# Two mixed layers of a float32 network: units reordered, heads taken in pairs between the k steps of gate units, convolution taps summed in PSUM

## The chip, the core and the metric

The kernel runs on one core of one Trainium2 chip. The metric is the device time of one execution in microseconds (us). The kernel before took 2114.37 us in the median of three runs (2113.19 to 2114.48).

## What is computed

A batch of one sequence of 256 tokens, width 1024, all float32, goes through two stacked networks. The first has two layers; each adds half a SwiGLU block (inner width 2816), then a hybrid mixer, then another half SwiGLU block. The second has a dilated attention mixer, a SwiGLU block, a forgetting attention mixer and a SwiGLU block. The change concerns the hybrid mixer alone, which runs twice:

```python
proj = h @ w_in + b_in                       # 1024 -> pa 1024 | pb 672 | pc 1024 | pg 3072
xa  = causal_conv4(pa[..., :512])            # LRU branch
y_a = (rg_lru(xa) * gelu(pa[..., 512:])) @ lru_w_out
q   = (rms_norm(cq) @ w_uq)                  # latent attention, 8 heads of 64 + 32 rotary
kv  = (rms_norm(ckv) @ w_ukv)
y_b = softmax_causal(q k^T) v @ mla_w_o
c   = pc[..., :512] * sigmoid(pc[..., 512:]) # convolution branch
c   = silu(layer_norm(causal_depthwise_conv31(c)))
y_c = c @ conv_w_out + conv_b_out
g   = sigmoid(pg)                            # three gates of width 1024
merged = g0 * y_a + g1 * y_b + g2 * y_c
x   = x + merged @ w_out
```

## The kernel before

**Weights.** All weights come in one stream of slots of 128 x 2048 float32 (1 MB) through three buffers. SyncE (SP) loads a slot into `raw` (`load`, L486 to L490) once the slot that had the buffer is split. ScalarE (ACT) rounds it to `whi` (`split`, L551 to L557), VectorE (DVE) makes `wlo = raw - whi` (L1018 to L1022), and TensorE (PE) forms each product as three float32r matmuls, hi x hi, hi x lo and lo x hi (`use`, L1794 to L1811). A slot is four k steps for both blocks of 128 rows: 24 matmuls of 512 columns. ACT may split slot i+2 as soon as PE is done with slot i-1.

**Order.** Every engine works through a list written out by hand, in order. ACT's and DVE's splits stand as `upto(i)` (all splits up to number i) between the other steps; where a step waits, all that stands behind it on its engine waits too. `MIX_UNITS` (L107) lists the products of a mixed layer (*units*), whose results go in turn to two pairs of PSUM banks, 0 and 1 and 2 and 3, so a unit can start when the one two before it has been read out. `MIX_TURNS` (L51) lists the groups of transposes (*turns*), which take banks 6 and 7 in turn in the same manner.

**A mixed layer.** It has 36 slots, in this order: `pa0`, `pa1` (the LRU branch's two inputs), `pb0`, `pb1` (latents), `glu`, `val` (the convolution branch's two), `uq0`, `uq1`, `uk`/`uv` (queries, keys, values), then for each branch its two gate units `g` and its two output units `y`, and last `wo0`, `wo1` (the output projection, L2184). PE's list is L2053 to L2191, ACT's L694 to L836, DVE's L1217 to L1424, POOL's (GpSimd's) L1659 to L1706. PE does the LRU gates' eight small matmuls in banks 4 and 5 (L2079), the turns of the query and key rows (`qk_turns`), and the eight heads in one run behind `g01` (`attention`, L1971 to L2043). For each head PE makes scores (L1984, L1986), DVE their largest value (L1126), ACT the exponentials with their row sums (L627), PE turns them (L1996), ACT copies them out (L618) and PE multiplies by the values (L2015), 64 columns a head. DVE divides all eight by the row sums at the end (L1119), and two more turns `o0`, `o1` bring the result to channels by tokens.

**The convolution.** It has 31 taps on 4 tiles of 128 channels x 256 tokens. DVE has tiles 0 to 2: `conv(n)` (L1228 to L1245) does n rounds of three `scalar_tensor_tensor`, with a drain ahead of each, which read the padded input and the sum in SBUF and write the sum in SBUF. POOL has tile 3: L1702 multiplies, L1705 adds, all 31 after `scan` and rotation (L1693 to L1706). PE then sums over channels for the mean and the variance (L2091).

**Gates and merging.** DVE reads out each gate unit with its bias (`biased`, L1247 to L1257) into one of two row buffers, ACT applies the sigmoid (L840), and `merge` (L1265 to L1290) multiplies an output unit by its gate and adds it to `merged`; for the third branch DVE first adds the output bias (L1281, L1284).

## Time and profile before

| what | value |
|---|---|
| median of three runs | 2114.37 us (2113.19 to 2114.48) |
| the profiled execution's own time | 2112.89 us |
| its span, first to last instruction | 2111.1 us |
| mean granted clock of TensorE | 0.985 |
| first mixed layer, from 199.5 to 464.0 us | 264.5 us |
| second mixed layer, from 837.4 to 1101.7 us | 264.3 us |

The profiled execution lies 1.8 us around its span and 1.5 us below the median. Its records of PE matmuls overlap: a matmul of 512 columns reads 0.39 us, and the next starts 0.23 us after it, so times of PE are read below from start to start and not from busy time. In the same manner VectorE's and ScalarE's records last longer than the distance to the next one.

### The profile page before, as it was taken

How to read it: one execution, taken by the hardware profiler on the slowest of the kernel's cores; microseconds unless marked ns; L12 is line 12 of the kernel's file. 1: busy time of each engine (PE TensorE's matmuls, PEld its weight loads, DVE VectorE, ACT ScalarE, POOL GpSimd, SP SyncE). 2: the span in 40 equal slices, each digit the busy share in tenths (PEclk: the TensorE clock that was granted, in tenths of full speed). 3: DMA queues.
4: the chain of work that ended last, by engine and by line, in shares of the span. 5: the costliest groups of instructions: out<-in, count | busy, mean ns of one | idle time of the engine just before them, and what ended most of it. 6: DMA issues, size and time to landing. Idle time of an engine off the chain costs nothing.

```text
span 2111.1 us, 26411 instructions
## 1 busy us (share of the span) xinstructions
PE 2035.4 (96%) x9851; PEld 1678.6 (80%) x9866; DVE 1238.3 (59%) x1366; ACT 1011.2 (48%) x1279; POOL 240.9 (11%) x357
## 2 busy tenths in 40 slices
PE   8999988999999999988999999999999999999998
PEld 6888867778888888867778887778778888888887
DVE  5555579865545555669865545555556455446554
ACT  5445664544445445664445444544445434455433
POOL 1000168000000000069000002111100000000000
PEclk9999998999999999999999999999999999999999
DMA  7554442545555555542455554444335554425552
GB/s 266 189 189 176 175 151 89 175 159 202 196 181 184 204 179 186 184 150 87 155 182 201 187 183 158 144 141 152 140 109 190 188 190 160 162 78 182 206 180 100
DMA packets 54626, 354.16 MB, mean 168 GB/s; under 512 B 7696, under 2 KB 8336, under 8 KB 12816
## 3 DMA queue, kind: packets, MB, share of 16 engines
q1 hardware_dynamic: 53968, 352.51, 47.1%
q8 instruction: 54, 0.88, 0.2%
q10 hardware_dynamic: 576, 0.53, 0.1%
q14 instruction: 28, 0.23, 0.0%
HBM read 351.97 MB, written 1.05 MB: 167 GB/s over the span
## 4 chain that ended last, share of the span: by engine, by line
PE 83%; DVE 7%; ACT 4%; DVEq 2%; issue 2%; POOL 1%; DMA 1%; POOLq 1%; SPq 0%; ACTq 0%
PE psum L1809 58%; PE psum L1860 17%; DVE wlo L1022 3%; DVE arena L1243 2%; ACT whi L557 2%; PE psum L1875 1%; DVEq L1237 1%; PE psum L1938 1%; PE psum L2230 1%; PE psum L2251 1%; DMA raw<-w_stream 1%; PE psum L2237 1%; PE psum L1821 1%; PE psum L2015 1%; POOL arena L1651 1%
## 5 line engine op out<-in xcount | busy, mean ns | idle before, releaser
L1022 DVE TENSOR_TENSOR wlo<-raw,whi 128x2048 fp32r<-128x2048 f32 x325 | 745.0, 2294 | 447.9 <-ACT whi L557 447.8
L1809 PE MATMUL psum<-whi,xTh 128*128 128x512 f32 (+1 forms) x1936 | 769.0, 397 | 14.8 <-DVE xTl L1048 5.2
L1809 PE MATMUL psum<-whi,xTl 128*128 128x512 f32 (+1 forms) x1936 | 752.9, 389 | 0.0
L1809 PE MATMUL psum<-wlo,xTh 128*128 128x512 f32 (+1 forms) x1936 | 752.8, 389 | 0.0
L557 ACT ACTIVATE whi<-raw 128x2048 fp32r<-128x2048 f32 x325 | 621.1, 1916 | 258.1 <-PE psum L1860 151.3
L1809 PEld LDWEIGHTS psum<-whi,xTh 128*128 128x128 f32 x1936 | 366.9, 190 | 93.2 <-issue 5.9
L1809 PEld LDWEIGHTS psum<-whi,xTl 128*128 128x128 f32 x1936 | 366.8, 189 | 76.3
L1809 PEld LDWEIGHTS psum<-wlo,xTh 128*128 128x128 f32 x1936 | 367.5, 190 | 69.4
L1860 PE MATMUL psum<-whi,braT 128*128 128x512 f32 x1056 | 337.7, 390 | 0.0
L1860 PEld LDWEIGHTS psum<-whi,braT 128*128 128x128 f32 x1056 | 198.3, 188 | 41.1
L1860 PE MATMUL psum<-wlo,braT 128*128 128x512 f32 x528 | 205.5, 389 | 0.0
L654 ACT ACTIVATE arena<-psum,small 128x256 f32<-128x256 f32 x132 | 55.4, 471 | 194.8 <-PE psum L1809 194.7
L659 ACT ACTIVATE braT<-psum 128x256 fp32r<-128x256 f32 x132 | 43.5, 382 | 217.2 <-PE psum L1875 217.2
L1165 DVE TENSOR_TENSOR braT<-psum,braT 128x256 fp32r<-128x256 f32 x132 | 49.9, 419 | 112.0 <-ACT braT L659 112.0
L1860 PEld LDWEIGHTS psum<-wlo,braT 128*128 128x128 f32 x528 | 99.2, 188 | 20.0
L1158 DVE SCALAR_TENSOR_TENSOR arena<-psum,small,arena 128x256 f32<-128x256 f32 x132 | 57.8, 480 | 85.0 <-ACT arena L654 84.6
L1243 DVE SCALAR_TENSOR_TENSOR arena<-arena,vec 128x256 f32<-128x256 f32 x180 | 98.7, 602 | 6.3 <-issue 1.8
L1702 POOL TENSOR_SCALAR arena<-arena,vec 128x256 f32<-128x256 f32 x60 | 77.2, 1287 | 0.3 <-issue 0.3
L1938 PE MATMUL psum<-con,arena 128*128 128x128 f32 (+2 forms) x372 | 52.7, 282 | 18.6 <-ACT arena L799 12.5
L1624 POOL TENSOR_SCALAR small<-small 128x2 f32<-128x2 f32 x9 | 1.7, 192 | 594.1 <-ACT arena L584 594.1
L1938 PEld LDWEIGHTS psum<-con,arena 128*128 128x128 f32 (+2 forms) x372 | 43.2, 136 | 28.9 <-ACT arena L799 13.5
L1809 PE MATMUL psum<-whi,latT 128*128 128x512 f32 (+1 forms) x176 | 57.3, 396 | 5.1 <-DVE wlo L1022 4.3
(236 smaller groups left out, 1449.2 us busy)
## 6 DMA issues: line engine op xcount, KB each, us to landing
raw<-w_stream SPq DMA_DIRECT2D x326, 1024.0 KB, 4.8
bias<-chunks SPq DMA_DIRECT2D x18, 256.0 KB, 5.0
x<-x_in SPq DMA_DIRECT2D x2, 512.0 KB, 5.1
raw<-w_stream SPq DMA_DIRECT2D x4, 256.0 KB, 7.3
arena<-gate_w SPq DMA_DIRECT2D x2, 512.0 KB, 5.1
arena<-fins SPq DMA_DIRECT2D x2, 512.0 KB, 5.8
con<-consts SPq DMA_DIRECT2D x1, 720.0 KB, 10.9
out<-x ACTq DMA_DIRECT2D x2, 256.0 KB, 2.3
```

The costliest lines, as they stand in the source:

```text
L557: act.activation(whi[:, r], raw[:, r], ACT.Copy).then_inc(hi_done, 1)
L654: act.activation(f_sg[:, rb], gate_up(b, j)[:, rb, 0:256], ACT.Silu, scale=rs[:, rb:rb + 1]).then_inc(silu_done, 1)
L659: act.activation(h_of(b, j, 0)[:, :, rb * P:(rb + 1) * P], psum[:, 6 + rb, 0:256].rearrange("p (t s) -> p t s", s=P), ACT.Copy).then_inc(t ...
L1022: TT(wlo[:, r], raw[:, r], whi[:, r].bitcast(F32), ALU.subtract).then_inc(lo_done, 1)
L1158: ins = STT(f_h[:, rb], gate_up(b, j)[:, rb, 256:512], rs[:, rb:rb + 1], f_sg[:, rb], ALU.mult, ALU.mult)
L1165: TT(h_of(b, j, 1)[:, :, rows], psum[:, 6 + rb, 0:256].rearrange("p (t s) -> p t s", s=P), h_of(b, j, 0)[:, :, rows].bitcast(F32), ALU.sub ...
L1237: dve.drain()
L1243: ins = STT(cacc[:, t], cpad[:, t, k:k + S], w, cacc[:, t], ALU.mult, ALU.add)
L1702: TS(products[:, k % 2, t - CONV_DVE], window, w, None, ALU.mult)
L1809: ins = pe.matmul(dst(rb), s(kt)[:, rows], w[:, r, at_:at_ + cols], start=start and n == 0 and k == 0, stop=stop and n == len(kts) - 1 and ...
L1860: ins = pe.matmul(pair(c)[:, rb], s[:, t, rows], w[:, r, t * D + c * W:t * D + (c + 1) * W], start=start and t == 0 and k == 0, stop=stop ...
L1938: ins = pe.transpose(dst[0:rows.shape[1], col:col + P], rows, ident)
```

## The change

- **Order of units.** `glu` and `val` come first, then `pa0`, `pa1`, `pb0`, `pb1`, `g00`, `uq0`, `uq1`, `uk`, `uv`, `g01`, `y00`, `y01`, `g10`, `g11`, `g20`, `g21`, and then `y10`, `y11`, `y20`, `y21` and the output projection. The weight stream is laid out to match. The turns follow, and `o0`, `o1` are gone.
- **Hooks.** Turns, scores, turns of probabilities, the products with the values, and the sums over channels are issued from hooks ahead of single k steps of the large units (`{4: [turn_p(0)], ...}`: number of k step and what stands before it).
- **Heads.** They go in four pairs. ACT also multiplies the probabilities by the reciprocal row sums (`normed`) before they are turned. The product with the values (`pv`) puts both heads of a pair into one bank with channels on the partitions, and ACT and DVE split it straight into `latT` (`o_hi`, `o_lo`).
- **Taps.** DVE's taps keep their sums in PSUM banks 4 and 5 and write SBUF only in the last round; they start after `val`. The LRU gates go to banks 6 and 7. POOL does 11 of its 31 taps ahead of the rotation and 20 after it.
- **Gate rows** have four buffers. The bias of the third branch times its gate is added to `merged` by POOL (`with_conv_bias`), not by DVE.
- **Output projection.** Its four slots go k half by k half (`wo0`, `wo1`, `wo0`, `wo1`). `uk`'s product signals on its own (`uk_in`).

The core of the diff:

```diff
-MIX_UNITS = [("pa0", 2, "act"), ("pa1", 2, "act"), ("pb0", 2, "dve"), ("pb1", 1, "dve"),
-             ("glu", 2, "act"), ("val", 2, "act"), ("uq0", 1, "act"), ("uq1", 1, "act"), ("uk", 1, "act"), ("uv", 0, "act"),
-             ("g00", 2, "dve"), ("g01", 2, "dve"), ("y00", 1, "dve"), ("y01", 1, "dve"),
-             ("g10", 2, "dve"), ("g11", 2, "dve"), ("y10", 1, "dve"), ("y11", 1, "dve"),
-             ("g20", 2, "dve"), ("g21", 2, "dve"), ("y20", 1, "dve"), ("y21", 1, "dve"),
+MIX_UNITS = [("glu", 2, "act"), ("val", 2, "act"), ("pa0", 2, "act"), ("pa1", 2, "act"), ("pb0", 2, "dve"), ("pb1", 1, "dve"),
+             ("g00", 2, "dve"), ("uq0", 1, "act"), ("uq1", 1, "act"), ("uk", 1, "act"), ("uv", 0, "act"),
+             ("g01", 2, "dve"), ("y00", 1, "dve"), ("y01", 1, "dve"),
+             ("g10", 2, "dve"), ("g11", 2, "dve"), ("g20", 2, "dve"), ("g21", 2, "dve"),
+             ("y10", 1, "dve"), ("y11", 1, "dve"), ("y20", 1, "dve"), ("y21", 1, "dve"),
...
+                def normed(p):
+                    act.wait_ge(mla_rden, M * MPAIRS + p + 1)
+                    for h in (2 * p, 2 * p + 1):
+                        for rb in range(RB):
+                            ins = act.activation(pm[h % 2][rb], pm[h % 2][rb], ACT.Copy, scale=rden[:, rb * NH + h:rb * NH + h + 1])
+                        ins.then_inc(mla_normed, 1)
...
+                def o_hi(p):
+                    act.wait_ge(mla_pv, M * MPAIRS + p + 1)
+                    act.activation(latT[:, 0, p], psum[:, 6, 0:S], ACT.Copy).then_inc(mla_hi, 1)
...
+                upto(15)
                 rows("uv", [v_row[:, rb] for rb in range(RB)], rs4[:, 2:4])
+                upto(16)
+                gate_sigmoid(b, 0)
                 act.wait_ge(ya_f, M + 1)
                 act.activation(braT[:, 0], gel, ACT.Copy).then_inc(ya_hi, 1)
                 upto(17)
+                qk_out(0)
+                qk_out(1)
+                upto(18)
+                qk_out(2)
+                qk_out(3)
                 gate_sigmoid(b, 1)
                 upto(19)
+                exp(0)
+                normed(0)
+                upto(20)
+                turned_out(0)
                 upto(21)
+                o_hi(0)
+                exp(1)
+                normed(1)
+                upto(22)
+                turned_out(1)
+                o_hi(1)
                 upto(23)
+                exp(2)
+                normed(2)
+                upto(24)
+                turned_out(2)
+                upto(25)
+                o_hi(2)
+                exp(3)
+                normed(3)
 
...
-                            w = vec_("dww", k * 4 + t)
+                            w, acc = vec_("dww", k * 4 + t), conv_acc(t)
                             if k == 0:
-                                ins = TS(cacc[:, t], cpad[:, t, 0:S], w, vec_("dwb", t), ALU.mult, ALU.add)
+                                if t == 0:
+                                    dve.drain()
+                                ins = TS(acc, cpad[:, t, 0:S], w, vec_("dwb", t), ALU.mult, ALU.add)
                             else:
-                                ins = STT(cacc[:, t], cpad[:, t, k:k + S], w, cacc[:, t], ALU.mult, ALU.add)
+                                ins = STT(cacc[:, t] if k == TAPS - 1 else acc, cpad[:, t, k:k + S], w, acc, ALU.mult, ALU.add)
                         if k == TAPS - 1:
                             ins.then_inc(conv_done, 1)
...
+                conv(1)
+                upto(5)
+                conv(2)
+                upto(6)
+                conv(2)
+                dve.wait_ge(xpad_in, M + 1)
+                lru_conv((0, 1))
+                upto(7)
+                lru_conv((2, 3))
+                upto(8)
+                conv(1)
+                upto(9)
+                conv(1)
+                biased("pb0", 0, [pb[:, rb, 0:W] for rb in range(RB)])
+                upto(10)
+                conv(1)
+                biased("pb1", 1, [pb[:, rb, W:] for rb in range(RB)])
+                dve.sem_inc(lat_row, 1)
+                upto(11)
+                conv(3)
+                for n, t0, tn in ((0, 0, 2), (1, 2, 1), (2, 3, 1), (3, 4, 1)):
+                    lo_turns(b, plan, f"lat{n}", latT[:, 1, t0:t0 + tn], latT[:, 0, t0:t0 + tn], [vec_("q_norm", t) for t in range(t0, t0 + tn)])
+                    if n == 1:
+                        conv(1)
+                        upto(12)
+                gate(0)
+                upto(13)
+                conv(1)
                 dve.wait_ge(sqrt_done, M + 1)
                 STT(gr, ltmp, 1.0, gr, ALU.add, ALU.mult)
+                upto(14)
                 dve.drain()
                 dve.wait_ge(ix_done, M + 1)
                 TT(gi, gr, gi, ALU.mult)
                 for t in range(4):
                     ins = dve.tensor_tensor_scan(gr[:, t], ltmp[:, t], gi[:, t], 0.0, ALU.mult, ALU.add)
                 ins.then_inc(scan_done, 1)
+                upto(15)
+                conv(3)
+                upto(16)
                 dve.wait_ge(ya_hi, M + 1)
                 TT(braT[:, 1], gel, braT[:, 0].bitcast(F32), ALU.subtract).then_inc(ya_lo, 1)
+                conv(1)
+                upto(17)
                 conv(2)
+                gate(1)
                 upto(18)
                 conv(2)
                 merge(0)
+                conv(1)
+                largest(0)
+                conv(1)
+                reciprocals(0)
                 upto(19)
+                conv(1)
                 merge(1)
+                upto(20)
+                conv(1)
+                o_lo(0)
+                upto(21)
+                largest(1)
+                conv(1)
+                reciprocals(1)
+                gate(2)
+                upto(22)
+                conv(1)
+                o_lo(1)
                 conv(2)
+                largest(2)
+                upto(23)
+                reciprocals(2)
+                gate(3)
+                upto(24)
                 conv(2)
+                o_lo(2)
+                conv(1)
+                largest(3)
                 upto(25)
+                reciprocals(3)
+                gate(4)
...
+                merge(2)
+                merge(3)
                 upto(30)
                 merge(4)
+                upto(31)
+                for n in range(2):
                     lo_turns(b, plan, f"m{n}", xTl[:, 2 * n:2 * n + 2], xTh[:, 2 * n:2 * n + 2])
+                merge(5)
+                upto(32)
+                upto(33)
+                for n in range(2, 4):
+                    lo_turns(b, plan, f"m{n}", xTl[:, 2 * n:2 * n + 2], xTh[:, 2 * n:2 * n + 2])
+                upto(34)
+                ready = lambda c, rb: dve.wait_ge(slot_used, b.slot + 35 + c)
                 residual(units.place("wo0"), 1.0, ready, ((0, 0), (0, 1)))
                 next_norm(b)
                 residual(units.place("wo0"), 1.0, ready, ((1, 0), (1, 1)))
...
+                def with_conv_bias(c):
+                    ch, g, cols = ROW_CHUNKS + c, g_row[:, G_BUFFER[4 + c]], slice(c * W, (c + 1) * W)
+                    per = sum(k % 3 == ch % 3 for k in range(len(CHUNKS)))
+                    wait(g_sig, M * 6 + 5 + c)
+                    wait(bias_in[ch % 3], M * (16 * per) + 16 * (ch // 3 + 1))
+                    TT(bias_g, over(bias[:, ch % 3], RB), g, ALU.mult)
+                    pool.drain()
+                    wait(merged_two, M * 2 + c + 1)
+                    TT(merged[:, :, cols], merged[:, :, cols], bias_g, ALU.add).then_inc(bias_merged, 1)
+                    pool.drain()
+
+                wait(tdve, b.tdve + plan.upto("val1", "split", "dve"))
+                taps(11)
...
+                def scores_of(p):
+                    def go():
+                        if p:
+                            pe.wait_ge(mla_lo, M * MPAIRS + p)
+                        else:
+                            turns_left(b, plan, "k3")
+                            pe.wait_ge(masks_done, 1)
+                        for h in (2 * p, 2 * p + 1):
+                            for rb in range(RB):
+                                keys, dst = (rb + 1) * P, mla_scores(h, rb)
+                                pe.matmul(dst, identb[:], maskb[:, (1 - rb) * P:2 * P], start=True, stop=False)
+                                ins = pe.matmul(dst, qT[0:QK, h, rb * P:(rb + 1) * P], kT[0:QK, h, 0:keys], start=False, stop=True)
+                            ins.then_inc(mla_s, 1)
+                    return go
+
+                def turn_p(p):
+                    def go():
+                        for h in (2 * p, 2 * p + 1):
+                            pe.wait_ge(mla_normed, M * MH + h + 1)
+                            for k, rows in enumerate((pm[h % 2][0], pm[h % 2][1][:, 0:P], pm[h % 2][1][:, P:])):
+                                ins = pe.transpose(psum[:, 6 + h % 2, k * P:(k + 1) * P], rows, ident)
+                            ins.then_inc(mla_turned, 1)
+                    return go
+
+                def pv(p):
+                    def go():
+                        if p == 0:
+                            pe.wait_ge(uact, b.uact + units.upto("uv", "act"))
+                        pe.wait_ge(mla_pt, M * MH + 2 * p + 2)
+                        for n, (kb, rb) in enumerate(((0, 0), (0, 1), (1, 1))):
+                            for half in range(2):
+                                h = 2 * p + half
+                                ins = pe.matmul(psum[half * VD:(half + 1) * VD, 6, rb * P:(rb + 1) * P], v_row[:, kb, h * VD:(h + 1) * VD],
+                                                ptm[half][:, n * P:(n + 1) * P], start=n < 2, stop=n != 1)
+                        ins.then_inc(mla_pv, 1)
+                    return go
+
...
+                proj("glu", 0, first=x_in_place)
+                proj("val", 2, {4: [glu_turns]})
+                proj("pa0", 4, {4: [val_turns]})
+                proj("pa1", 6, {4: [lx]})
+                proj("pb0", 8, {4: [gelu_]})
+                gates(0)
+                whole(b, units, "pb1", 10, 1, QR + KVR + ROPE - W, xh, xl, never, k_per_slot=KT)
+                gates(1)
+                proj("g00", 11, {4: [lambda: latents(0)], 6: [lambda: latents(1)]})
...
+                proj("g01", 16, {4: [rope_ready, qk_turn("q", 0)], 5: [qk_turn("k", 0)], 6: [qk_turn("q", 1)], 7: [qk_turn("k", 1)]})
+                pe.wait_ge(ya_lo, M + 1)
+                branch(0, 18, braT, {0: [qk_turn("q", 2)], 1: [qk_turn("k", 2)], 2: [qk_turn("q", 3)], 3: [qk_turn("k", 3)]})
+                branch(1, 19, braT, {1: [scores_of(0)]})
+                proj("g10", 20, {3: [turn_p(0)], 5: [pv(0)], 7: [scores_of(1)]})
+                proj("g11", 22, {4: [turn_p(1)], 6: [pv(1)]})
+                proj("g20", 24, {0: [scores_of(2)], 4: [turn_p(2)], 6: [pv(2)]})
+                proj("g21", 26, {0: [scores_of(3)], 1: [means], 4: [turn_p(3)], 5: [variances], 6: [pv(3)]})
+
+                def pair_out(kt):
+                    pe.wait_ge(mla_lo, M * MPAIRS + kt + 1)
+
+                branch(2, 28, latT, first=pair_out)
+                branch(3, 29, latT)
                 pe.wait_ge(yc_lo, M + 1)
                 branch(4, 30, braT)
+
+                def first_half():
+                    pe.wait_ge(merged_done, M * 2 + 1)
+                    row_turns(b, plan, ("m0", "m1"), merged)
+
+                branch(5, 31, braT, {3: [first_half]})
...
+                for kt in range(4):
+                    out(0, kt)
+                out(1, 0)
+                pe.wait_ge(merged_done, M * 2 + 2)
+                row_turns(b, plan, ("m2", "m3"), merged[:, :, W:])
+                for kt in range(1, 4):
+                    out(1, kt)
+                for kt in range(4, 8):
+                    out(0, kt)
+                out(1, 4)
+                out(1, 5)
+                norm_turns(b.next)
+                out(1, 6)
+                out(1, 7)
```

## Rows read from the trace of the kernel before

**Rows 1.** The page: busy time by engine (first line), chain that ended last (second).

```profile
PE 2035.4 (96%) x9851; PEld 1678.6 (80%) x9866; DVE 1238.3 (59%) x1366; ACT 1011.2 (48%) x1279; POOL 240.9 (11%) x357
...
PE psum L1809 58%; PE psum L1860 17%; DVE wlo L1022 3%; DVE arena L1243 2%; ACT whi L557 2%; PE psum L1875 1%; DVEq L1237 1%; PE psum L1938 1%; PE psum L2230 1%; PE psum L2251 1%; DMA raw<-w_stream 1%; PE psum L2237 1%; PE psum L1821 1%; PE psum L2015 1%; POOL arena L1651 1%
```

**Rows 2.** Busy time by stretch: both mixed layers, then five stretches of the first.

```profile
core 0: us, PE busy (x) PEld busy (x) DVE busy (x) ACT busy (x) POOL busy (x), PEclk, DMA share, GB/s
199.50:464.00 264.50, 240.24 (x1143) 198.67 (x1142) 199.87 (x250) 143.41 (x188) 88.20 (x92) 0.95 0.43 152
837.40:1101.70 264.30, 238.66 (x1142) 196.61 (x1141) 199.46 (x249) 143.01 (x188) 88.20 (x92) 0.96 0.43 152
267.50:286.50 19.00, 15.14 (x70) 12.57 (x69) 13.30 (x13) 14.41 (x17) 7.93 (x7) 0.91 0.71 248
297.50:346.10 48.60, 35.66 (x201) 29.92 (x200) 46.79 (x74) 24.33 (x55) 45.51 (x42) 0.86 0.27 93
346.10:358.70 12.60, 12.60 (x50) 10.28 (x50) 12.28 (x19) 5.35 (x4) 11.86 (x12) 0.86 0.26 83
381.40:404.40 23.00, 20.69 (x88) 16.02 (x87) 21.65 (x24) 9.14 (x6) 0.00 (x0) 1.00 0.69 236
432.20:457.70 25.50, 20.47 (x88) 16.36 (x89) 16.53 (x13) 9.49 (x8) 0.00 (x0) 0.93 0.34 124
```

**Rows 3.** TensorE's waits in the first mixed layer: line, releaser: us, times, longest.

```profile
PE psum L1938 <- ACT arena L799: 6.3, 2, 5.1
PE psum L1984 <- ACT arena L627: 5.5, 2, 2.7
```

**Rows 4.** Timeline of TensorE: start us, us, line, operation; large matmuls and one turn.

```profile
217.79 0.39 PE L1809 MATMUL psum<-wlo,xTh 128*128 128x512 f32 x1
...
228.49 1.03 PE L1938 MATMUL psum<-con,arena 128*128 128x128 f32 x8
229.28 0.48 PE L1809 MATMUL psum<-whi,xTh 128*128 128x512 f32 x1
229.59 0.40 PE L1809 MATMUL psum<-wlo,xTh 128*128 128x512 f32 x1
```

**Rows 5.** Timeline of TensorE: scores of two heads, values of two heads.

```profile
314.06 0.31 PE L1984 MATMUL psum<-maskb,identb 128*128 128x128 bf16 x1
...
316.27 0.59 PE L1809 MATMUL psum<-whi,xTh 128*128 128x512 f32 x1
...
344.68 1.70 PE L2015 MATMUL psum<-arena 128*128 128x64 f32 x12
346.14 0.78 PE L1809 MATMUL psum<-whi,braT 128*128 128x512 f32 x1
```

**Rows 6.** Timeline of POOL: both rotations start, the product with `gel`.

```profile
279.16 3.69 POOL L1651 TENSOR_TENSOR arena<-arena,mcos 128x128 f32<-128x128 f32 x1 [5.96 <-ACT arena L721]
...
287.42 2.51 POOL L1651 TENSOR_TENSOR arena<-arena,mcos 128x128 f32<-128x128 f32 x1
...
292.17 2.39 POOL L1691 TENSOR_TENSOR arena<-arena 128x1024 f32<-128x1024 f32 x1
```

**Rows 7.** Groups of ACT, first mixed layer: count | busy us, mean ns | idle before.

```profile
L557 ACT ACTIVATE whi<-raw 128x2048 fp32r<-128x2048 f32 x37 | 70.3, 1912 | 27.2 <-PE psum L1809 23.9 <-DMA raw<-w_stream 2.8 <-issue 0.5
L721 ACT ACTIVATE arena<-psum,small 128x512 f32<-128x512 f32 (+1 forms) x16 | 9.6, 660 | 8.3 <-PE psum L1809 8.3
```

**Rows 8.** Groups of DVE, first mixed layer, same columns.

```profile
L1022 DVE TENSOR_TENSOR wlo<-raw,whi 128x2048 fp32r<-128x2048 f32 x37 | 84.9, 2294 | 46.1 <-ACT whi L557 46.0
L1243 DVE SCALAR_TENSOR_TENSOR arena<-arena,vec 128x256 f32<-128x256 f32 x90 | 49.4, 602 | 3.2 <-issue 0.9
```

**Rows 9.** Timeline of DVE: a round of taps beside POOL; four operations that read PSUM.

```profile
303.35 1.88 DVE L1243 SCALAR_TENSOR_TENSOR arena<-arena,vec 128x256 f32<-128x256 f32 x3
305.15 2.28 DVE L1022 TENSOR_TENSOR wlo<-raw,whi 128x2048 fp32r<-128x2048 f32 x1
...
277.55 1.65 DVE L1340 SCALAR_TENSOR_TENSOR arena<-psum,vec,arena 128x256 f32<-128x256 f32 x4
279.12 2.28 DVE L1022 TENSOR_TENSOR wlo<-raw,whi 128x2048 fp32r<-128x2048 f32 x1
```

More of the change, by code:

```diff
@@ new lines, in mix @@
+                act.wait_ge(lat_row, M + 1)
+                for n, (c0, c1) in enumerate(((0, QR), (QR, QR + KVR))):
+                    for rb in range(RB):
+                        act.activation(junk[:, 0:c1 - c0], pb[:, rb, c0:c1], ACT.Square, accum_out=ss4[:, 2 * n + rb:2 * n + rb + 1])
+                        act.drain()
+                act.sem_inc(lat_ss, 1)
+                upto(13)
+                act.wait_ge(lat_r, M + 1)
+                rows("uq0", [q_row[:, rb, 0:4] for rb in range(RB)], rs4[:, 0:2])
@@ L2116, in mix @@
-                for name, at_ in (("uk", 0), ("uv", W)):
-                    unit_free(b, units, name)
-                    u = units.place(name)
-                    ins = use(b, 13, [(3 + k, k * D + at_) for k in range(2)], W, lath, latl, never, lambda rb: pair(u)[:, rb], True, True)
-                ins.then_inc(slot_used, 1)
-                proj("g00", 14)
-                pe.wait_ge(rope_q, M + 1)
-                pe.wait_ge(rope_k, M + 1)
-                pe.wait_ge(uact, b.uact + units.upto("uk", "act"))
@@ new lines, in mix @@
+                pe.wait_ge(tdve, b.tdve + plan.upto("lat3", "split", "dve"))
+                for name, at_, done in (("uk", 0, uk_in), ("uv", W, slot_used)):
+                    unit_free(b, units, name)
+                    u = units.place(name)
+                    ins = use(b, 15, [(3 + k, k * D + at_) for k in range(2)], W, lath, latl, never, lambda rb: pair(u)[:, rb], True, True)
+                    ins.then_inc(done, 1)
+                proj("g01", 16, {4: [rope_ready, qk_turn("q", 0)], 5: [qk_turn("k", 0)], 6: [qk_turn("q", 1)], 7: [qk_turn("k", 1)]})
@@ new lines, in mix, with out @@
+                branch(5, 31, braT, {3: [first_half]})
+                def out(c, kt):
+                    if kt % 2 == 0 and c == 0:
+                        pe.wait_ge(tdve, b.tdve + plan.upto(f"m{kt // 2}", "split", "dve"))
+                    if kt == 0:
+                        unit_free(b, units, f"wo{c}")
+                    ins = use(b, 32 + 2 * (kt // 4) + c, [(kt, (kt % 4) * W)], W, xh, xl, never,
+                              lambda rb: pair(units.place("wo0") + c)[:, rb], kt == 0, kt == 7)
+                    if kt % 4 == 3:
+                        ins.then_inc(slot_used, 1)
@@ L2437, in mix @@
         pg0 = pc0 + 2 * CONV
+        yield from unit(w, pc0 + W, pc0 + 2 * W)
+        yield from unit(w, pc0, pc0 + W)
         yield from unit(w, 0, W)
```

435 lines of the change are left out of this document (192 added, 243 removed).

## The prediction

> **What bounds the kernel now.** I read the page first: TensorE is busy 96% of the span, DVE 59%, ACT 48%, and the chain that ended last runs through PE's weight matmuls for the most part [rows 1]. So a gain has to come from time in which PE doesn't work at its pace, and busy time hides that, since its records overlap. Its pace is read from starts: from 217.79 to 228.49 us stand 47 matmuls of 512 columns, 0.227 us each, and a turn of eight transposes takes 0.79 (228.49 to 229.28) [rows 4]. A slot of 24 matmuls is 5.45 us.
>
> Next, busy time by stretch, which gives a mixed layer 264.5 and 264.3 us [rows 2]. The five stretches below them hold the loss; I take the work in each at the pace above. `uq0` to `uv`, 19.0 us: 36 matmuls of 384 columns (0.17, by the width), 24 of 512 and 8 transposes are 12.4, so 6.6 is lost. The turns of queries and keys, `g01` and all heads, 48.6 us: 32 + 24 transposes 5.5, 48 matmuls 10.9, four times two heads' scores 8.8 (2.21 from 314.06 to 316.27) and 48 value passes 5.8 (1.46 for 12) [rows 5] are 31.0; lost 17.6. `y00` and `y01`, 12.6: 10.9; lost 1.7. `y10` to the first half of `g20` with both channel sums, 23.0: 72 matmuls 16.3 and the 16 passes of the channel sums (the rest of the 88 counted), taken at 0.22 like a matmul of 512, 3.5; lost 3.2. The output projection, 25.5: 72 matmuls and 16 transposes, 17.9; lost 7.6. Together **36.7 us in a layer**. The granted clock says the same: 0.91, 0.86, 0.86 and 0.93 in four of the five stretches, so part of each loss is PE at 1.2 GHz behind a wait. The waits themselves name what PE waited for: query and key copies 6.3, exponentials 5.5 [rows 3]. Both stand behind ACT's and DVE's lists, and DVE is busy 46.8 of 48.6 us there, so **DVE bounds that stretch** [rows 2].
>
> **The change, part by part.**
>
> *Taps in PSUM.* A round of three taps beside POOL takes 1.80 us (303.35 to 305.15); 90 taps fill 49.4 us at a mean of 602 ns [rows 8, 9]. No row shows DVE writing PSUM. From below: four operations of the same size that read PSUM and one SBUF tensor start 0.39 apart (277.55 to 279.12 for four), with records of 0.48 (1.65 less three times 0.39). From above: the contended round, 0.60 a tap. I take 0.40, since the new taps differ from the nearest row only in where they write: 90 x 0.40 is 36, so 13 us of DVE go in each layer, at the bound none. By the Trainium skill (SBUF — State Buffer, Who interferes with whom), a VectorE instruction contends with GpSimd only if two of its tensor inputs lie in SBUF; rows 9 agree. The same skill (VectorE: DVE Perf Modes, The TRN2 errata) gives PSUM sources 62 cycles more than SBUF sources, which speaks against the change: as an estimate by that page 0.065 us a tap, 6 us of DVE a layer. Rows 9 speak against that page: a PSUM source starts its next as soon as 0.39.
>
> *Other DVE work.* The bias addition goes to POOL (2.4), two operations at the heads' end and two of `o0`, `o1` go (2.6), four `o_lo`, eight small reciprocals come (about 3). With the taps, DVE falls from 200 [rows 2] to some 185 us. ACT gains 16 copies for `normed`, some 6 us, on 143. POOL gains four passes like the 2.39 of rows 6 at the tail. None of them is a bound; each is covered while PE's slots last.
>
> *Splits as cover.* ACT may split slot i+2 at the end of slot i-1, 10.9 us before use; the two splits take 1.9 and 2.3 [rows 7, 8]. So ACT and DVE may come 6.7 us late with everything that stands ahead of a split. SP's loads and the ten bias chunks are issued behind DVE's splits, and their new places ask for bias buffers freed more than a slot before.
>
> *The new order, walked* with these durations, from the layer's start. `glu` to `pb1`: every turn's input is ready one slot ahead; no wait. Both latent splits lie inside `g00`. `uq0` starts at 79.4; `uk`'s slot is split at 84.5 and needed at 85.9; `g01` at 91.0 against 91.4. So 6.6 becomes about 0, with 0.4 to 1.4 in hand. *Rotation:* POOL starts it when ACT has read out `uq1` (0.66 a block [rows 7]), at 86.9. It took 13.0 us before (279.16 to 292.17, 8.3 for the first block of rows and 4.8 for the second) [rows 6] and again meets DVE's splits and scans: ready at 99 to 100, while `g01`'s second half is due at 96.9. That is a **wait of 2.7**. Then ACT stands at `ya_f`, which needs POOL's 2.39 more, and behind it its split and the copies of `q0`, `k0`: `q1`'s turn waits till 105.5 instead of 103, **2.3**. DVE holds its lo of `y00` behind the same signal, in time. *Heads:* scores of pair 0 end at 120.4, maxima 122.1, exponentials 124.0, `normed` 126.0, `turn_p` at 128.6. For pair 2 the chain ends at 159.2 against 160.2, the tightest. All values and their splits fit too, by 1 to 3 us. DVE's taps end at 166.0, POOL's at about 150, means at 171: no wait. *Tail:* DVE merges both halves of branches two and three behind one another, slot 31 is split at 202.4 against 202.9; `m0`'s lo makes **0.5**. POOL's bias products stand just ahead of `merge(4)` (about 203.5 against 204.6); uncovered they cost their 2.4.
>
> *Taken off PE:* eight transposes of `o0`, `o1`, 0.8. *Added:* some 16 more changes between large and small matmuls at 0.08 (229.28 to 229.59 against 0.227) [rows 4], 1.5. *Clock:* a wait of this size near `g01` may again bring a stretch at 1.2 GHz; the stretches of rows 2 lost about half of such time; I take 1.7, between none and 3.4. *For what no row shows* (queue order inside a slot) 0.8, between none and 5.
>
> **Sum, a layer:** 36.7 + 0.8 - 1.5 - 2.7 - 2.3 - 0.5 - 1.7 - 0.8 = 28.0, less the 1.0 of the other small waits that a layer keeps: 27.0. Twice is 54. The profiled execution's 2112.9 becomes 2058.9; its median stands 1.5 higher, so I forecast **2060 us**.
>
> **Rivals.**
>
> 1. *PSUM taps are no cheaper* than contended ones (upper bound). DVE keeps 13 us more a layer, spread over slots 5 to 25; the tight places (`uk`, `g01`, pair 2) turn into waits of 1 to 2 us each, some 5 a layer: 2070. For it: no row writes PSUM. Against: rows 9. By the rule of the Trainium skill's page VectorE: DVE Perf Modes (62 cycles more for a PSUM source) about half of that would come, 2065 as an estimate from that page.
> 2. *Late hooks.* Each pair has two tight hooks (`turn_p`, `pv`) behind ACT's and DVE's lists. If the eight come 1.5 us late, 12 a layer are lost: 2084. For it: DVE is still near full between slots 17 and 25. Against: the splits give 6.7 of slack, and no pair has more than one hook with under 1.7 in hand.
> 3. *No stall left*: POOL rotates sooner because DVE's taps leave it alone, and the clock holds. Then 5.0 + 0.5 + 1.7 + 0.8 comes back a layer: 2044.
> 4. *Slower than before.* PE's queue is in order, so a hook that waits holds the k steps behind it, which before ran free of the heads. Twelve hooks a layer (`scores`, `turn_p`, `pv`) would have to wait over 2.3 us each beyond the walk to eat 27; from there it decides the sign. The chain of a pair would then last 17 us against the 11 to 13 of two slots; at 3 us each the time is 2132. Against: its members sum to about 9.
> 5. *Nothing happens*: the loss of 36.7 moves behind other waits and the time stays 2113. Against: the heads' run, which DVE bounds, no longer exists as a run.
>
> **How the numbers follow.** Forecast 0.56 (own range 2051 to 2068), rival 1 0.12, rival 2 0.14, rival 3 0.12, rival 4 0.04, rival 5 0.02. A measurement of this kernel tells 0.2%, some 4 us, from no change. Faster 0.94, same 0.02, slower 0.04. The range takes in rivals 1 to 3 but their last microseconds: 2045 to 2085.
>
> **What would show it.** Right: taps at 0.47 to 0.49 us in every record, also beside POOL; both layers at 237 us from `glu` to the next block; PE's granted clock above 0.98 in them; waits left on POOL's rotation and on ACT's query copies. Wrong: taps above 0.55 (rival 1), waits of `turn_p` on `normed` or of `pv` on ACT's copies over 1 us each (rivals 2, 4), no wait on the rotation (rival 3). A tail that still loses over 3 us would say that the merges' order was misjudged.

## The result, and the profile after

The changed kernel takes **2061.8 us** (median of 4 runs, 2060.5 to 2063.1) against 2114.0 for the kernel before: a ratio of 0.975, 95% interval 0.974 to 0.9765. The forecast was 2060. The profiled span is 2060.7 us, 50.4 less than before.

The page of the changed kernel, busy time and chain:

```profile
PE 2013.2 (98%) x9835; PEld 1660.3 (81%) x9850; DVE 1234.6 (60%) x1374; ACT 1021.5 (50%) x1313; POOL 292.0 (14%) x365
...
PE psum L1924 65%; PE psum L1975 17%; PE psum L2053 2%; PE psum L1990 1%; PE psum L2393 1%; PE psum L2414 1%; DVEq L1347 1%; PE psum L2400 1%; PE psum L1936 1%; PE psum L2254 1%; PE psum L2101 0%; POOL arena L1752 0%; DVE wlo L1090 0%; ACT whi L574 0%; DMA raw<-w_stream 0%
```

DVE's splits were 3% of the chain [rows 1] and round to 0% now. DVE's total has hardly moved, which hides two opposite changes shown below. Busy time by stretch: both mixed layers, the rotation and `g01`, and the tail:

```profile
199.50:438.40 238.90, 227.38 (x1136) 188.04 (x1135) 196.28 (x254) 148.14 (x205) 113.57 (x96) 0.99 0.48 168
811.60:1049.40 237.80, 229.13 (x1136) 188.93 (x1135) 195.80 (x253) 147.54 (x205) 113.61 (x96) 0.99 0.46 168
267.50:311.00 43.50, 38.32 (x190) 31.86 (x189) 42.05 (x53) 34.44 (x51) 32.95 (x31) 1.00 0.53 188
394.00:412.00 18.00, 11.67 (x55) 9.21 (x53) 17.72 (x9) 7.54 (x6) 14.00 (x4) 0.99 0.35 117
```

Counted from the start of a layer's first large matmul to that of the next block's, the two layers went from 264.6 and 264.7 us to 238.8 and 237.8, and the granted clock in them from 0.95 and 0.96 to 0.99. ([rows 2] cut the second layer at 837.4 and 1101.7; by the starts it runs from 837.1 to 1101.9.) They gain 25.8 and 26.9. The rest of the program, which the change does not touch, is 2.3 longer in this execution, nearly all of it behind the second layer; why is open. What TensorE still waits for in the first layer:

```profile
PE psum L1924 <- DVE wlo L1090: 3.9, 2, 3.1
PE psum L2053 <- DVE arena L1348: 3.2, 1, 3.2
PE psum L2053 <- issue: 2.5, 1, 2.5
PE psum L2053 <- ACT arena L791: 1.9, 1, 1.9
```

The waits on exponentials [rows 3] are gone, and no score, turn of probabilities or value of the heads waits. The last two rows are the forecast waits in `g01`. "Issue" is the one ahead of the first q turn, which starts at 300.63; the other ends at 306.31. From start to start they cost 2.6 and 2.0 us. (The expectations below call them by 292.5 and 302.8, where the stretches with these waits begin.) The first two rows lie in the tail (the last output units and the output projection), except 0.85 us of the first, which is ahead of `uk` at 287.0. DVE's groups in the first layer:

```profile
L1090 DVE TENSOR_TENSOR wlo<-raw,whi 128x2048 fp32r<-128x2048 f32 x36 | 90.3, 2511 | 22.5 <-ACT whi L574 21.4 <-issue 1.0
L1313 DVE SCALAR_TENSOR_TENSOR psum<-arena,vec,psum 128x256 f32<-128x256 f32 x87 | 36.9, 484 | 2.5
L1348 DVE TENSOR_TENSOR arena<-arena 128x1024 f32<-128x1024 f32 x4 | 6.6, 1660 | 0.4
```

A tap in PSUM takes 484 ns on average (479 to 492 in all 174 records, beside POOL too), where it was 602 [rows 8]. But the splits grew from 2294 to 2511 ns each: DVE's load fell on one side and rose on the other. The timeline of DVE and then of POOL in the tail shows where more than half of that came from, 4.4 of 7.8 us (start us, us):

```profile
396.71 2.13 DVE L1348 TENSOR_TENSOR arena<-arena 128x1024 f32<-128x1024 f32 x1
398.76 8.87 DVE L1090 TENSOR_TENSOR wlo<-raw,whi 128x2048 fp32r<-128x2048 f32 x2
407.55 1.21 DVE L1346 TENSOR_TENSOR arena<-psum,arena 128x1024 f32<-128x1024 f32 x1
408.85 2.06 DVE L1348 TENSOR_TENSOR arena<-arena 128x1024 f32<-128x1024 f32 x1
```

```profile
395.00 2.75 POOL L1786 TENSOR_TENSOR arena<-bias,arena 128x1024 f32<-128x1024 f32 x1 [42.00 <-ACT arena L908]
397.99 3.08 POOL L1789 TENSOR_TENSOR arena<-arena 128x1024 f32<-128x1024 f32 x1 [0.24 <-issue]
401.42 4.06 POOL L1786 TENSOR_TENSOR arena<-bias,arena 128x1024 f32<-128x1024 f32 x1 [0.35 <-issue]
405.72 4.11 POOL L1789 TENSOR_TENSOR arena<-arena 128x1024 f32<-128x1024 f32 x1 [0.24 <-issue]
```

Two splits fill 8.87 us instead of some 4.5. Each began while a POOL pass was running, and both finished late. The adds of L1348 take 2.1 where the PSUM-reading products of L1346 keep 1.2. Starts of TensorE's matmuls say what it cost: 8.1 us in the first layer, 7.4 in the second. Waits are 6.6 and 5.6 of these. Most of the rest is TensorE's clock, which fell behind them: some 1.4 and 1.6 us of matmuls at 1.2 GHz. It fell once more behind the rotation's wait in the second layer, which cost another 1.6, and not in the first. The stretches, with the granted clock third from the end:

```profile
411.00:414.70 3.70, 3.70 (x15) 3.12 (x16) 3.31 (x3) 1.20 (x2) 0.00 (x0) 0.60 0.40 124
1015.90:1019.50 3.60, 3.60 (x10) 2.81 (x9) 3.60 (x1) 0.00 (x0) 3.36 (x2) 0.53 0.78 291
912.00:918.00 6.00, 5.39 (x20) 4.12 (x20) 5.85 (x10) 3.12 (x3) 5.85 (x5) 0.72 0.47 175
302.00:308.00 6.00, 4.15 (x23) 3.17 (x22) 5.91 (x7) 4.42 (x5) 5.80 (x4) 1.00 0.45 153
```

### The profile page after: what moved, and what is told of

It is laid out like the page before. It is cut to its first block, busy times and chain, and to the rows that moved or that the text cites. A ratio compares the mean times of both kernels' runs of the same rounds, so it can differ in the third digit from the quotient of the medians.

```text
span 2060.7 us, 26397 instructions
## 1 busy us (share of the span) xinstructions
PE 2013.2 (98%) x9835; PEld 1660.3 (81%) x9850; DVE 1234.6 (60%) x1374; ACT 1021.5 (50%) x1313; POOL 292.0 (14%) x365
## 4 chain that ended last, share of the span: by engine, by line
PE 91%; ACT 3%; DVE 2%; POOL 1%; DVEq 1%; issue 1%; POOLq 1%; DMA 0%; SPq 0%; ACTq 0%
PE psum L1924 65%; PE psum L1975 17%; PE psum L2053 2%; PE psum L1990 1%; PE psum L2393 1%; PE psum L2414 1%; DVEq L1347 1%; PE psum L2400 1%; PE psum L1936 1%; PE psum L2254 1%; PE psum L2101 0%; POOL arena L1752 0%; DVE wlo L1090 0%; ACT whi L574 0%; DMA raw<-w_stream 0%
## 5 line engine op out<-in xcount | busy, mean ns | idle before, releaser
L1090 DVE TENSOR_TENSOR wlo<-raw,whi 128x2048 fp32r<-128x2048 f32 x325 | 760.4, 2342 | 400.1 <-ACT whi L574 397.9
L1975 PE MATMUL psum<-whi,braT 128*128 128x512 f32 x1056 | 337.8, 390 | 0.0
L1313 DVE SCALAR_TENSOR_TENSOR psum<-arena,vec,psum 128x256 f32<-128x256 f32 x174 | 73.8, 484 | 5.0
L1776 POOL TENSOR_TENSOR arena<-arena 128x256 f32<-128x256 f32 x60 | 66.6, 1110 | 8.8
L1924 PE MATMUL psum<-whi,braT 128*128 128x512 f32 x160 | 58.2, 426 | 8.3 <-DVE wlo L1090 6.2
```

What stands on the lines that cost most here:

```text
L1090: TT(wlo[:, r], raw[:, r], whi[:, r].bitcast(F32), ALU.subtract).then_inc(lo_done, 1)
L1313: ins = STT(cacc[:, t] if k == TAPS - 1 else acc, cpad[:, t, k:k + S], w, acc, ALU.mult, ALU.add)
L1776: ins = TT(cacc[:, CONV_DVE], cacc[:, CONV_DVE], ctap[:, k % 2], ALU.add)
L1924: ins = pe.matmul(dst(rb), s(kt)[:, rows], w[:, r, at_:at_ + cols], start=start and n == 0 and k == 0, stop=stop and n == len(kts) - 1 and ...
L1975: ins = pe.matmul(pair(c)[:, rb], s[:, t, rows], w[:, r, t * D + c * W:t * D + (c + 1) * W], start=start and t == 0 and k == 0, stop=stop ...
```

## The experiments

Medians are of four runs each. Theory and rival are as they were put before the run; compare with 2061.8. The kernel before, measured again beside them, took 2113.4 to 2114.6, so a step of about 1 us between two of these medians says nothing.

**Taps back in SBUF**

```diff
 def conv_acc(t):
-    return psum[:, 4 + t // 2, (t % 2) * S:(t % 2 + 1) * S]
+    return cacc[:, t]
```

> The changed kernel with one part undone: VectorE's convolution taps accumulate in SBUF again, all else as changed. Theory (the sum of the forecast): a tap costs 0.60 us there as in the kernel before instead of the 0.484 us that the changed kernel's trace shows, so 87 taps a layer bring VectorE back some 10 us, and the rounds beside GpSimd's taps more; VectorE is 82% busy over the layer (196.3 of 238.9 us), so a part of it shows: 2 to 6 us a layer, 2066 to 2074 us, most of it between 267 and 311 us, where VectorE is 97% busy. Rival (the layer has cover enough, the order alone is the gain): 2062 us like the changed kernel, within 1.5.

Measured: **2077.7** (ratio 0.983, 0.981 to 0.9845). That is 8 us a layer, above both the theory's range and the rival's. The group of the taps, first layer:

```profile
L1313 DVE SCALAR_TENSOR_TENSOR arena<-arena,vec 128x256 f32<-128x256 f32 x90 | 50.6, 614 | 2.6
```

New waits are spread over the layer: latent splits 1.1, `g01`'s bank (`biased`, L1324) 1.8, the scores of a pair on `o_lo` 1.2; the granted clock between 311 and 330 us is 0.91. In starts, 2.1 us are lost up to 311 us, where the theory had most of it, and 5.8 behind. So some 12 us of DVE work bring 8 of time: the new order leaves little slack between 267 and 346 us. Without the PSUM taps it still gains 18 us a layer.

**The heads together**

```diff
-branch(1, 19, braT, {1: [scores_of(0)]})
-proj("g10", 20, {3: [turn_p(0)], 5: [pv(0)], 7: [scores_of(1)]})
...
+branch(1, 19, braT)
+proj("g10", 20, {0: [scores_of(0), turn_p(0), pv(0)]})
+proj("g11", 22, {0: [scores_of(1), turn_p(1), pv(1)]})
+proj("g20", 24, {0: [scores_of(2), turn_p(2), pv(2)]})
+proj("g21", 26, {0: [scores_of(3), turn_p(3), means, pv(3)], 5: [variances]})
```

> The changed kernel with the spreading of the heads undone: each pair's scores, turns and values stand at one place, the first k step of a gate unit, with nothing between them, as TensorE's own order; all else as changed. Theory (the gain of this part is that k steps cover maximum, exponential, reciprocal, normalisation and copy of a pair): each of four pairs leaves TensorE idle for the chain of VectorE and ScalarE steps, which the trace of the kernel before prices at some 6 to 9 us beside splits, so 24 to 36 us a layer less what the other engines catch up meanwhile: 2105 to 2125 us. Rival (the idle time only moves, since VectorE and ScalarE are what bounds the stretch and their work is the same): under 10 us a layer, 2062 to 2080 us.

Measured: **2137.8** (1.011, 1.0095 to 1.013), 38 us a layer, above the theory's 2125 too: **1.1% slower than the kernel before**. TensorE's waits in the first layer, then its busy time over the four pairs:

```profile
PE psum L2263 <- ACT arena L774: 13.8, 4, 3.9
PE psum L2275 <- ACT arena L782: 10.0, 4, 5.0
```

```profile
320.00:408.00 88.00, 64.18 (x286) 49.17 (x284) 45.42 (x75) 33.17 (x69) 28.08 (x28) 0.78 0.26 101
```

Those two waits are 23.8 of the 38. The rest lies beside them: the granted clock of the stretch is 0.78, so matmuls behind a wait ran partly at 1.2 GHz. The rival falls, since DVE is busy 45.4 of 88 us there. The old kernel didn't run pairs like this: it let one head's scores overlap the next one's turns. So 38 us is the price of pairs without cover, not the gain over the old way.

**POOL's taps left out of the kernel before**

```diff
-for k in range(TAPS):
+for k in range(2):
     for t in range(CONV_DVE, 4):
```

> The kernel before with 29 of GpSimd's 31 convolution rounds left out (part of the convolution is not computed), so that VectorE works alone there. It asks how much of the old loss at the heads and behind them was contention between the two engines, which the new order could win by starting those rounds earlier. Theory of the forecast (the stretch was bound by VectorE's own amount of work and by units that stood back to back): 2105 to 2114 us, at most 4 us a layer. Rival (contention was the larger part of the loss): 2080 to 2100 us.

This kernel leaves 29 of POOL's 31 rounds out, so it computes only a part of the convolution. Measured: **2093.6** (0.990, 0.989 to 0.992), 10 us a layer less than the kernel before and in the rival's band. My theory put at most 4 on contention. The group of DVE's taps, first layer:

```profile
L1243 DVE SCALAR_TENSOR_TENSOR arena<-arena,vec 128x256 f32<-128x256 f32 x90 | 38.3, 481 | 3.1 <-issue 0.9
```

The same instruction, reading two SBUF tensors, takes 481 ns with POOL quiet, 602 with POOL beside it [rows 8], and 484 into PSUM whatever POOL does. So what PSUM taps save is, within 3 ns a tap, what POOL's company cost. The rule of the Trainium skill that speaks against the change (VectorE: DVE Perf Modes, The TRN2 errata: 62 cycles more for a PSUM source, 0.065 us by estimate) isn't seen: the changed kernel's taps of the last round, with a PSUM source and SBUF out, take 473 to 481 ns. The Trainium skill's rule on who shares (SBUF — State Buffer, Who interferes with whom: two SBUF inputs contend with GpSimd, one does not) agrees with the three numbers, 481, 602 and 484.

**The third branch's bias back on DVE, and POOL's passes in pieces**

In `merge` for n of 4 and more, and at the end of POOL's program:

```diff
-dve.wait_ge(bias_merged, M * 2 + c + 1)
-TT(g, y, g, ALU.mult).then_inc(udve, 1)
...
+TT(bias_g, y, over(bias[:, ch % 3], RB), ALU.add).then_inc(udve, 1)
+dve.drain()
+TT(g, bias_g, g, ALU.mult)
...
-with_conv_bias(0)
-with_conv_bias(1)
```

> The changed kernel with the third branch's bias on VectorE again (y plus bias, times gate, plus merged: three passes in each of two merges), and none of GpSimd's four passes of 128x1024. Theory (a long GpSimd instruction that already runs holds VectorE's splits to 4.46 us instead of 2.29): the splits at 394 and 399 us fall back to 2.3 us, TensorE's 8.1 us of waits between 394 and 412 us shrink to at most 4 a layer although VectorE has two passes more, and the kernel takes 2050 to 2056 us. Rival (the tail is bound by the amount of VectorE's work behind merge 2 and 3, not by GpSimd): two passes of some 1.1 to 1.2 us more a layer's half make it 2064 to 2071 us.

Measured: **2051.1** (0.970, 0.969 to 0.972), in the theory's range. The tail's stretch and DVE's timeline in it:

```profile
394.00:412.00 18.00, 16.17 (x74) 12.60 (x73) 17.57 (x14) 9.92 (x8) 0.00 (x0) 1.00 0.46 173
```

```profile
396.40 1.23 DVE L1354 TENSOR_TENSOR arena<-arena 128x1024 f32<-128x1024 f32 x1
397.54 4.49 DVE L1090 TENSOR_TENSOR wlo<-raw,whi 128x2048 fp32r<-128x2048 f32 x2
401.95 1.22 DVE L1348 TENSOR_TENSOR arena<-psum,bias 128x1024 f32<-128x1024 f32 x1
```

DVE has one pass more in each half and is faster: the two splits take 4.49 instead of 8.87, the add 1.23 instead of 2.13. The tail loses 2.5 us in place of 8.1.

Against that, POOL keeps the work and both its passes are cut up (the second in the same way as the first):

```diff
+pieces = [(rb, slice(n * S, (n + 1) * S)) for rb in range(RB) for n in range(2)]
-TT(bias_g, over(bias[:, ch % 3], RB), g, ALU.mult)
+for rb, of in pieces:
+    TT(bias_g[:, rb, of], bias[:, ch % 3, of], g[:, rb, of], ALU.mult)
```

> The changed kernel with GpSimd's four bias passes of 128x1024 cut into sixteen of 128x256, the same work in the same place. Theory (it is the length of the one GpSimd instruction that holds a split): a split waits at most for one piece of some 0.7 to 1.1 us, so the two splits of 4.46 us fall to about 3, and 3 to 5 us of the 8.1 a layer go: 2052 to 2057 us. Rival (while GpSimd has such work the two share the port whatever the pieces): the splits stay over 4 us, 2060 to 2064 us.

Measured: **2060.7** (0.975, 0.9735 to 0.977): the rival's time, by another road. DVE and POOL in the tail:

```profile
397.76 5.57 DVE L1090 TENSOR_TENSOR wlo<-raw,whi 128x2048 fp32r<-128x2048 f32 x2
406.13 1.22 DVE L1346 TENSOR_TENSOR arena<-psum,arena 128x1024 f32<-128x1024 f32 x1 [2.79 <-POOL arena L1792]
```

```profile
394.92 6.27 POOL L1788 TENSOR_TENSOR arena<-bias,arena 128x256 f32<-128x256 f32 x4 [42.16 <-ACT arena L908]
401.43 4.57 POOL L1792 TENSOR_TENSOR arena<-arena 128x256 f32<-128x256 f32 x4 [0.24 <-issue]
```

The splits do fall, to 2.8 each, so it is the length of POOL's instruction that sets how long they are held. But now POOL is held: four pieces take 6.27 where one pass took 2.75, and `merge(4)` waits 2.79 for them. Short pieces hand the delay from DVE to POOL; here both lead to the same merge.

**The waits in `g01`**

ACT's copy of the first turns ahead of its wait:

```diff
 gate_sigmoid(b, 0)
+qk_out(0)
 act.wait_ge(ya_f, M + 1)
 act.activation(braT[:, 0], gel, ACT.Copy).then_inc(ya_hi, 1)
 upto(17)
-qk_out(0)
 qk_out(1)
```

> The changed kernel with one step of ScalarE's order moved: the copy of the first q and k turns stands ahead of its wait on GpSimd's gated branch, not behind it. Theory (that wait of 4.5 us is what holds the second q turn, 2.1 us on TensorE at 302.8 us in the first mixed layer and 0.9 in the second): 1.5 to 3 us less in all, 2058.5 to 2060.5 us. Rival (what the turn loses there comes back at the next k turn or at the branch that waits for the same GpSimd product): within 1 us of the changed kernel.

Measured: **2059.8** (0.975, 0.973 to 0.976), 2.0 less, as the theory put it, though the lowest and highest runs of the two kernels overlap (2058.6 to 2061.4 against 2060.5 to 2063.1). The wait ahead of the q1 turn is gone in both layers, where it was 2.0 and 0.4 in starts. But in the first layer TensorE's clock now falls behind the rotation's wait (0.84 granted between 302 and 308 us), which costs 1.6. Up to the q1 turn that layer gains only 0.5.

The traces say why so little is to be won here. In the changed kernel, `bias_dve`, `bias_pieces`, `ix_dve` and `taps_sbuf` one of the two layers keeps the full clock behind the rotation's wait, and ACT's copies hold the q1 turn for 1.8 to 2.0 us. The other runs a few us partly at 1.2 GHz and reaches that turn late, so its wait is 0.2 to 0.4. Each layer pays one or the other.

The rotation on POOL in halves, where `rotate_half(n)` waits for `uq{n}` and turns its four heads in both row blocks; the first q turn waits for the first half and the k part, the q2 turn for the second half:

```diff
+rotate_half(0)
...
 ins.then_inc(rope_k, 1)
-wait(uact, b.uact + units.upto("uq1", "act"))
-for rb in range(RB):
...
+rotate_half(1)
```

> The changed kernel with GpSimd's rotation of the q rows in two halves of four heads: the first right behind uq0, before the copies of the k part, the second behind uq1; the first q turn waits for the first half and the k part alone. Theory (the 2.6 us of TensorE at 292.5 us in each layer is the wait for the whole rotation, which ends at 300.5): the first half and the copies end at some 294 to 297 us and the wait goes; the gated product behind the second half comes 1 to 3 us later and the second q turn's wait on ScalarE grows by a part of that: 2057 to 2060 us. Rival (twice as many GpSimd instructions beside VectorE's splits cost more than the halves give): 2062 to 2068 us.

Measured: **2074.4** (0.9815, 0.980 to 0.983), far over the rival's 2068. The wait ahead of the q1 turn went from 1.9 to 7.5. TensorE's longest wait of the first layer, and POOL's timeline:

```profile
PE psum L2058 <- ACT arena L791: 7.5, 1, 7.5
```

```profile
284.83 2.38 POOL L1749 TENSOR_TENSOR arena<-arena,mcos 128x64 f32<-128x64 f32 x1
287.18 0.32 POOL L1750 TENSOR_TENSOR arena<-arena,msin 128x64 f32<-128x64 f32 x1
...
302.28 2.44 POOL L1755 TENSOR_TENSOR arena<-arena 128x64 f32<-128x64 f32 x1
```

A piece of 64 columns needs 0.32 us alone and 2.4 when it meets a split. The last one met one (it began at 302.26), the gated product came 4.2 us later (304.7 against 300.5), and ACT, which stands at `ya_f`, held the copy that `q1`'s turn needs. The first q turn did gain 1.7. The mechanism was right and the price not: what stands behind the moved work decides.

**Products on DVE, and versions put together**

The product of gate and convolved input goes from POOL to DVE, ahead of DVE's wait on `sqrt_done`:

```diff
+dve.wait_ge(gates_out, M * 2 + 2)
+TT(gi, gi, xa, ALU.mult)
```

> The changed kernel with one GpSimd pass of 128x1024 moved to VectorE: the product of input gate and convolved input (2.40 us on GpSimd at 282.3 us, and the split that stood beside it took 4.32 us). Theory (a long GpSimd pass costs VectorE more than the same pass does on VectorE): VectorE pays 1.2 us and gets 2.0 back from that split, GpSimd's rotation ends 2.4 us or more earlier, TensorE's 2.6 us at 292.5 us in each layer go: 2054 to 2058 us. Rival (VectorE is 97% busy there, so a pass more delays the splits, and the rotation stretches beside them all the same): 2061 to 2066 us.

Measured: **2061.2** (0.975, 0.973 to 0.977), the rival. The split that stood beside this product did fall, from 4.32 to 2.30 us, and paid for the added pass. The changed kernel's DVE and POOL, and then DVE in this run:

```profile
282.54 4.32 DVE L1090 TENSOR_TENSOR wlo<-raw,whi 128x2048 fp32r<-128x2048 f32 x1 [0.26 <-issue]
...
282.32 2.40 POOL L1807 TENSOR_TENSOR arena<-arena 128x1024 f32<-128x1024 f32 x1
```

```profile
282.17 2.30 DVE L1090 TENSOR_TENSOR wlo<-raw,whi 128x2048 fp32r<-128x2048 f32 x1 [0.26 <-issue]
...
285.75 1.22 DVE L1436 TENSOR_TENSOR arena<-arena 128x1024 f32<-128x1024 f32 x1
```

But POOL only stood idle for 2.56 us: the rotation can't start before `uq1` is read out (287.29 against 287.68), and meets the same splits and scans; it ends 0.7 us earlier.

`best1` is `bias_dve` with `act_order` and `rot_early`; `best2` is `bias_dve` with `ix_dve` and `act_order`; `best3` is `bias_dve` with `ix_dve` and the gated product on DVE too; `best4` is `best3` with `rot_early`. The gated product's move:

```diff
 ins = dve.tensor_tensor_scan(gr[:, t], ltmp[:, t], gi[:, t], 0.0, ALU.mult, ALU.add)
-ins.then_inc(scan_done, 1)
+dve.drain()
+TT(gel, gr, gel, ALU.mult).then_inc(ya_f, 1)
```

> The changed kernel with three edits together: the bias on VectorE, ScalarE's copy ahead of its wait, the rotation in halves. Theory (the waits are three different ones, so the gains add): 2051.1 less 2 and less 3 to 5, 2044 to 2048 us. Rival (with the first two waits gone the units of the next stretch find VectorE, 97% busy there, late instead, and give them back): 2049 to 2052 us.

> The changed kernel with the bias on VectorE, that product on VectorE too, and ScalarE's copy ahead of its wait. Theory: 2051.1 us less what ix_dve wins and 1 to 2 for ScalarE's order, 2042 to 2048 us. Rival (the waits between 279 and 311 us hand on to one another, as with the rotation in halves): 2049 to 2053 us.

> The changed kernel with the bias and both products of 128x1024 that stood on GpSimd around the rotation on VectorE. Theory (GpSimd's work of any length near splits costs more than it takes over): the gated branch is ready some 5 us earlier, so ScalarE's wait of 4.5 us and the second q turn's wait go as well, VectorE has 1.2 us more: 2040 to 2047 us. Rival (VectorE's own amount of work binds between 267 and 311 us): 2050 to 2056 us.

> The changed kernel with the bias and both products of 128x1024 on VectorE, and the rotation in halves on GpSimd, which now is idle for 2.5 us ahead of the first half. Theory (with the gated branch no longer behind the rotation, the later second half delays only the q2 turn, which has slack): the first q turn no longer waits, 3 us a layer less than with the two products alone: 2044 to 2048 us. Rival (every GpSimd instruction that meets a split takes 2.3 to 2.5 us whatever its size, so twice as many of them end as late): 2050 to 2056 us.

Measured: 2056.3 (above the rival's band, as `rot_early` would have it), **2049.6** and 2052.0 (the rivals'), and **2049.3** (0.969, 0.9675 to 0.971; between the two). No theory here held. Nearly all that was won is the bias on DVE. `best2` and `best4` bring 1.5 and 1.8 us on top, less than the 0.2% that such a comparison tells, and `best1` and `best3` lose 5.2 and 0.9. That fits waits and clock around `g01` that hand on to one another, which no run shows by itself. `bias_dve`, `best2` and `best4` are all faster than both kernels; `bias_dve` is the simplest.

## Why the prediction was right, and where it was not

The sum came out within 2 us, and that is partly luck: two of its terms were wrong in opposite directions.

- **Taps.** Right: 479 to 492 ns, 0.40 between starts. The bound below was the value, and the reason (one SBUF source isn't disturbed) is what the runs show. Rows 9 could not show it: their four PSUM-reading operations ran while POOL stood idle (its next instruction is that of 279.16 in rows 6), so "rows 9 agree" read too much into them. What I hadn't seen is how much of the old loss was this contention: with POOL's taps gone, the old order alone was 10 us a layer faster. Rival 1 was also priced too low: its 5 a layer measured 8. DVE's total was to fall from 200 to 185 and is 196, since its splits and other passes with two SBUF inputs grew beside POOL.
- **Spreading the heads.** Right: no hook of the heads waits, so rivals 2 and 4 fell. The price of the same heads without cover is 38 us a layer, so the new order pays only with its hooks.
- **Heads, cheaper than taken.** The stretch was costed with 2.21 us for two heads' scores and 1.46 for 12 value passes [rows 5]. TensorE's timeline of after has 1.58 and 0.81:

```profile
318.69 0.23 PE L2253 MATMUL psum<-maskb,identb 128*128 128x128 bf16 x1
...
320.27 0.59 PE L1924 MATMUL psum<-whi,braT 128*128 128x512 f32 x1
...
332.12 0.88 PE L2275 MATMUL psum<-arena 128*64 128x128 f32 x12
332.93 0.50 PE L1924 MATMUL psum<-whi,xTh 128*128 128x512 f32 x1
```

  Four times 0.63 and 0.65 is 5.1 us a layer that the forecast left as work. The scores of rows 5 stood at a mean granted clock of 0.72 (314.0 to 316.5 in before), so that row was no price at full clock; I should have looked at its clock before taking it. The value passes were at 0.97; those changed form, which my walk passed over.
- **The waits in `g01`.** Right in place and cause: 2.7 and 2.3 forecast, 2.6 and 2.0 measured in the first layer. In the second the q1 turn's wait is only 0.4, and the clock costs 1.6 there. Rival 3 falls.
- **`uq0` to `uv`.** "So 6.6 becomes about 0" was 1.1 us short, for the tail's reason: `uk`'s slot had 1.4 us in hand with a split taken at 2.3, and that split met POOL's product of 282.32 and took 4.32. In `ix_dve`, where it takes 2.30, the wait ahead of `uk` falls from 0.9 to 0.3.
- **The tail failed.** The step that failed is "slot 31 is split at 202.4 against 202.9; `m0`'s lo makes 0.5", with POOL's four passes taken as covered. It measured 8.1 and 7.4. I had priced what POOL's passes cost POOL, not what they cost DVE while they ran: I used 2.3 us for a split and 1.2 for an add beside them. `bias_dve` shows the term: without them the tail loses 2.5. The prediction had said that a tail losing over 3 would mean misjudged merges. The order of the merges is the same in `bias_dve`, so that reading of its own sign was wrong as well.
- **Clock and the unshown.** The clock's 1.7 was right in kind: some 1.4 us in the first layer, all in the tail, and 3.2 in the second, half of it near `g01` where it was expected. Of the 0.8 for what no row shows I find nothing.
- **The ledger.** By the starts, the forecast for both layers is 237.6 and 237.7. The tail adds 7.6 and 6.9 (its clock included) and `uk` 1.1. Cheaper heads take off 5.1 and `g01` 0.4 (its clock included). The 2.5 set aside for clock and the unshown come off too, since the clock is counted with the waits here. That gives 238.3 and 237.7; measured are 238.8 and 237.8.
- **What stays open.** No run undoes the new order of units, the split of POOL's taps, the four gate buffers or the order of the output projection by itself. The kernel before with PSUM taps in the old order wasn't run either; without POOL's taps that order gained 10 us a layer.

## What to carry to other kernels

Before moving a long pass to GpSimd because it is idle, look at what VectorE runs beside it: here four GpSimd passes (14.0 us of records) beside instructions with two SBUF sources cost TensorE 5.6 us in the first layer, while VectorE does the same with one added pass of 1.2 us in each half. An accumulator in PSUM took VectorE's taps out of that contention, at no price per instruction (484 ns against 481). And a small chain with three engines in it belongs between k steps of a large product; for a moved step, follow what is queued behind it before its price is believed.

## What was not expected of the hardware

- A VectorE split that meets GpSimd passes of 128x1024 took 4.46 and 4.48 us instead of 2.29; beside pieces of 128x256, 2.8. A GpSimd instruction of 0.32 us took 2.4 when it met a split. The later one's record grew by about what was left of the one running: the split of 398.76 by 2.2 us, with 2.3 left of the POOL pass of 397.99.
- Twelve value passes that write two 64-row halves of one PSUM bank in turn take 0.81 us, 0.067 each, where the old 12 passes of 64 columns into 128 rows took 1.46. What makes the difference wasn't tried by itself.
- Behind one and the same wait of 2.6 us, TensorE's clock fell in one layer and not in the other (0.72 against 1.00 granted, in the stretches above), so a trace of one layer does not tell what such a wait costs.
